# Rows of the experts gathered on TensorE by products with a 0/1 matrix, and a third set of expert weights in the space of keys and values

## What is computed

```python
t = h.reshape(-1, 1024)                           # 384 tokens
grp_gate, grp_idx = top_k(softmax(t @ moe_wg + moe_bg), 1)        # 1 of 4 groups
sel = (t @ moe_we + moe_be) of that group                         # 8 experts in a group
top_p, top_i = top_k(softmax(sel), 2)                             # 2 of the 8
w = grp_gate * top_p / sum(top_p)
for e in range(32):
    y = (silu(t @ w_gate[e]) * (t @ w_up[e])) @ w_down[e]         # hidden size 256
    acc += combine[:, e] * y
```

## Time and profile before

| what | value |
|---|---|
| median of 3 runs | 1150.37 us (1147.16 to 1150.96) |
| profiled execution, its own time | 1151.86 us |
| its span | 1150.1 us |
| PE busy / DVE / ACT / POOL | 970.8 / 487.3 / 332.5 / 138.0 us |
| mean granted clock of TensorE | 0.926 of full speed |
| DMA moved | 302.08 MB, mean 263 GB/s |
| chain that ended last | PE 51%, DMA 26%, DVE 14% |
| line of the chain with most | PE L666 26%, then the DMA of `moe_w_up` 24% |

### The profile page before, as it was taken

How to read it: one execution, slowest core, us unless ns; L and a number is a source line. 1 busy time by engine, 2 the same in 40 slices (tenths; PEclk the granted TensorE clock), 3 DMA queues, 4 the chain that set the end, 5 groups by cost and what they waited for, 6 DMA issues and landing times.

```text
span 1150.1 us, 20717 instructions
## 1 busy us (share of the span) xinstructions
PE 970.8 (84%) x7674; PEld 646.0 (56%) x7674; DVE 487.3 (42%) x1271; ACT 332.5 (29%) x879; POOL 138.0 (12%) x193
## 2 busy tenths in 40 slices
PE   5899888999468788788879999998964887888887
PEld 3456655655345455455558888776543554555454
DVE  2079876521632333333430314685145332333334
ACT  3211353530522222221330101575132222222222
POOL 0400140000400010000010055000022100010000
PEclk8999999999679999988979999998976999999998
DMA  9999736772269999999873323100215799999993
GB/s 353 279 316 361 254 110 234 264 271 74 101 229 374 416 416 417 419 418 418 337 257 110 96 87 129 56 1 2 78 69 219 298 416 417 416 417 417 417 418 126
DMA packets 84913, 302.08 MB, mean 263 GB/s; under 512 B 5541, under 2 KB 34449, under 8 KB 68465
## 3 DMA queue, kind: packets, MB, share of 16 engines
q1 hardware_dynamic: 81584, 291.03, 65.4%
q0 software_dynamic: 2832, 8.61, 2.6%
q10 hardware_dynamic: 432, 1.57, 0.3%
HBM read 291.87 MB, written 9.32 MB: 262 GB/s over the span
## 4 chain that ended last, share of the span: by engine, by line
PE 51%; DMA 26%; DVE 14%; ACT 3%; issue 3%; SPq 1%; POOL 1%; POOLq 0%; DVEq 0%; ACTq 0%
PE banks L666 26%; DMA ring<-in_moe_w_up_dram 24%; PE banks L978 6%; PE banks L675 5%; DVE a L1508 5%; PE banks L1022 4%; PE banks L973 4%; DVE a L1443 2%; PE banks L704 2%; PE banks L1001 1%; DVE rt L1443 1%; SPq L561 1%; DMA bc<-in_moe_be_dram 1%; PE banks L949 1%; POOL bc L2041 1%
## 5 line engine op out<-in xcount | busy, mean ns | idle before, releaser
L666 PE MATMUL banks<-ring,hT 128*128 128x256 f32 (+1 forms) x720 | 153.9, 376 | 1.7 <-ACT hT L1164 1.6
L666 PEld LDWEIGHTS banks<-ring,hT 128*128 128x128 f32 x720 | 135.0, 191 | 21.3 <-DMA ring<-in_ev_w_in_dram 1.9
L1216 ACT ACTIVATE a<-banks 32x256 f32<-32x256 f32 (+1 forms) x208 | 88.3, 425 | 199.0 <-PE banks L1001 100.5
L1539 DVE SCALAR_TENSOR_TENSOR xT<-banks,mod,xT 128x128 f32<-128x128 f32 x352 | 118.7, 409 | 63.0 <-PE banks L1022 63.0
L1022 PE MATMUL banks<-a 128*128 128x384 f32 x352 | 134.0, 527 | 3.5 <-ACT a L1216 3.3
L1443 DVE TENSOR_TENSOR a<-a,banks 64x128 f32<-64x128 f32 (+1 forms) x64 | 21.7, 340 | 268.9 <-ACT a L1199 268.9
L666 PE MATMUL banks<-hT,ring 128*128 128x384 f32 x384 | 127.9, 493 | 1.6 <-ACT hT L1164 1.6
L978 PE MATMUL banks<-ring,a 128*32 128x128 f32 x2560 | 92.1, 304 | 43.1 <-DMA ring<-in_moe_w_up_dram 42.5
L978 PEld LDWEIGHTS banks<-ring,a 128*32 128x32 f32 x2560 | 80.5, 122 | 69.5 <-issue 68.4
L973 PE MATMUL banks<-ring,a 128*64 128x256 f32 x704 | 85.7, 398 | 25.5 <-DMA ring<-in_moe_w_up_dram 20.4
L666 PEld LDWEIGHTS banks<-hT,ring 128*128 128x128 f32 x384 | 73.1, 192 | 53.5 <-issue 3.8
(11 more groups left out here) (262 smaller groups left out, 1038.3 us busy)
## 6 DMA issues: line engine op xcount, KB each, us to landing
ring<-in_moe_w_gate_dram SPq DMA_DIRECT2D x64, 1024.0 KB, 8.7
ring<-in_moe_w_up_dram SPq DMA_DIRECT2D x64, 1024.0 KB, 10.8
ring<-in_moe_w_down_dram SPq DMA_DIRECT2D x64, 1024.0 KB, 10.3
ring<-in_ada_w_dram SPq DMA_DIRECT2D x44, 1024.0 KB, 8.4
ring<-in_od_w_qkv_dram SPq DMA_DIRECT2D x12, 1024.0 KB, 5.5
ring<-in_ev_w_in_dram SPq DMA_DIRECT2D x6, 1024.0 KB, 12.8
a<-sorted_rows SPq DMA_DIRECT2D x12, 512.0 KB, 6.8
a<-in_ada_w_dram SPq DMA_DIRECT2D x4, 1024.0 KB, 17.6
```

The lines of the kernel that those rows point to most:

```text
L666: mm = pe.matmul(out, lhsT, rhs, start=(k == 0), stop=(k == len(pairs) - 1))
L1216: ins = act.activation(y_pair[q % BUFFERS][row:row + rows, width * b:width * b + width], work[3][rows * b:rows * b + rows, 0:width], ACT.Copy)
L1539: ins = ve.scalar_tensor_tensor(out=xT[:, c, a:b], in0=work_banks(l)[pair + k][:, a:b], scalar=mcol(l, 5, c, j), in1=xT[:, c, a:b], op0=AL ...
```

## The change

- The rows of a tile are gathered from `htok` on PE: for each of 8 chunks of channels, three products (one for each 128 tokens) with `picks`, a matrix of 0 and 1 that says which token stands in which row of the tile. Two halves of 12 products, both through `work[0]`; DVE copies half 0, ACT half 1 into `teT`.
- `picks` of tile 0 is made by DVE during routing, from expert and rank alone; those of tiles 1 to 10 by POOL, from the codes that routing makes anyway (six comparisons of 128x128 and one addition of 128x384 for a tile).
- `sorted_rows`, its scatter, its loads, `pad_stored`, the prefix sum, `starts` and POOL's copy for each expert go.
- `AHEAD` = 3: the weights of experts 2, 5, 8 ... go to `a23` (`beside_ring`), the others stay in `ring`; expert n is loaded when expert n-3 is done. Expert 2 is fixed in the first place of the sorted ones and loaded before the order is known, once the first output product of the mixer is done.
- The loop body stays at six steps, with 3 turns in place of 4; six more steps are written out.

```diff
+AHEAD = 3
-BODIES = (NE - 1 - STEPS_AHEAD) // UNROLL
+BODIES = (NE - 1 - STEPS_AHEAD) // UNROLL - 1
...
+        def expert_slot(l, n, k):
+            return beside_ring[k] if n % AHEAD == AHEAD - 1 else slot(expert_piece(l, n, k))
...
 (SP, expert_loads)
-                            sp.wait_ge(sem(used), BUFFERS * t + (NE * l + n - 1))
+                            sp.wait_ge(sem(used), AHEAD * t + (NE * l + n - AHEAD + 1))
...
-                for n in range(BUFFERS):
-                    weights(n, 0, False)
-                sp.wait_ge(sem("rows_sorted"), 16 * 2 * NT * (l + 1))
-                for i, rows in enumerate(sorted_in):
-                    sp.dma_start(rows, sorted_rows[P * i:P * i + P, :]).then_inc(sem(f"sorted{i}_loaded"), 16)
+                weights(0, 0, (0, 1))
+                is_filled(sp, ("out", l, 0))
+                sp.wait_ge(sem("cache_stored"), 32 * (l + 1))
+                weights(AHEAD - 1, 0)
+                weights(0, 0, (2,))
+                weights(1, 0)
                 sp.wait_ge(sem("order_ready"), l + 1)
...
 (PE, routing)
+                pe.wait_ge(sem("first_picked"), l + 1)
+                is_read(pe, ("htok", l, NT - 1, 1))
+                gather(opened(("rows", l, 0)), 0, 0).then_inc(sem("filled"), 1)
                 out = opened(("lead", l))
                 pe.wait_ge(sem("counts_compared"), l + 1)
                 product(out[0:NE, 0:2], [(outranks[0:NE, :], ones[0:NE, 0:2])])
-                product(out[0:NE, 2:4], [(below[0:NE, 0:NE], count_col[0:NE, :])])
                 product(out[:, NE:2 * NE], [(ones[0:NE, :], outranks[0:NE, :])], True)
+                gather(opened(("rows", l, 1)), 0, 1).then_inc(sem("filled"), 1)
...
+            def gather(out, q, half):
+                for c in range(4):
+                    for t in range(NT):
+                        mm = pe.matmul(out[:, P * c:P * c + P], htok[:, t, 4 * half + c:D:KD], picks[:, q % 2, t, :],
+                                       start=(t == 0), stop=(t == NT - 1))
+                return mm
...
 (PE, step)
                     q, i = group_step(n)
-                    if i:
+                    if i == 0:
+                        gather_half(q + 2, 0, t)
+                    else:
                         spread_out(q, ((0, 1), (2, 3))[i - 1], t)
+                        if i == 1:
+                            gather_half(q + 2, 1, t)
                     down(n - 1, t)
+                def second_step():
+                    gate_up(1)
+                    await_hid(0)
+                    hid_turn(0)
+                    gather_half(1, 0)
+                    down(0)
+                    gather_half(1, 1)
+                    pe.wait_ge(sem("diagonals_ready"), l + 1)
+                    for i in range(NT):
+                        pe.matmul(work[4 + i], ones[:, :], diagonals[:, 4 * i:4 * i + 4, :], start=True, stop=True).then_inc(sem("codes_filled"), 1)
...
 (DVE, routing; the prefix sum and the places are left out)
+                for t in range(NT):
+                    ins = ve.tensor_scalar(picks[:, 0, t, :], lane, fixed[:, t:t + 1], None, ALU.is_equal)
...
                 link(ve.memset(key_col[0:STATIC, :], -1e6))
+                link(ve.memset(key_row[:, STATIC:STATIC + 1], 4e6))
...
 (POOL)
-                    link(pool.memset(a7[0:ROWS, 0:D], 0.0))
-                    pool.dma_start(sorted_rows[PAIRS:PAIRS + ROWS, :], a7[0:ROWS, 0:D]).then_inc(sem("pad_stored"), 16)
-                    pool.wait_ge(sem("pad_stored"), 16)
...
+                pool.wait_ge(sem("codes_found"), l + 1)
+                for q in range(1, TILES):
+                    if q == 2:
+                        is_filled(pool, ("rows", l, 1))
+                    elif q > 2:
+                        pool.wait_ge(sem("rows_gathered"), 2 * (GROUPS * l + q - 2))
+                    if GROUPS * l + q > 1:
+                        pool.wait_ge(sem("picked"), GROUPS * l + q - 1)
+                    for i in range(2 * NT):
+                        ins = pool.tensor_scalar(equal[:, i, :], lane, pick_codes[:, q - 1, i:i + 1], None, ALU.is_equal)
+                    link(ins)
+                    ins = pool.tensor_tensor(out=picks[:, q % 2, :, :], in0=equal[:, 0:NT, :], in1=equal[:, NT:2 * NT, :], op=ALU.add)
+                    ins.then_inc(sem("picked"), 1)
```

## The result

The changed kernel takes **1248.78 us** (1246.15 to 1257.1, 4 runs), the kernel before 1149.51 (1147.16 to 1150.96, 4 runs): a ratio of 1.0878 [1.0824, 1.0933]. The forecast was 1135, with 1149 as its upper end, so it had the wrong sign, by 114 us. The profiled execution took 1248.54 us, 1246.8 of them span.

A forecast was written before the change was run, and what follows sets the result against it. DMA was taken to bound the experts' steady part, with PE close behind. 1151.86 - 3.3 (pad) - 10 (experts, both layers) - 2 (layer ends) = 1136.6, median 1.5 lower: 1135 us, range 1120 to 1149.

The forecast's parts named there:

- part 3: Steady expert groups: with the gather a group takes 23.3 us against DMA's 22.61; experts -5.0 us a layer, start included.
- I take 0.12: 5.8 us for a tile, 2.88 for each half: Gather on PE in the steady groups: 48 records a tile at 0.12 us each.
- PE's weight loads do not hide: Rival, gather's strided weight loads: 0.16 to 0.19 us a record, kernel 1170 to 1195 us; chance 0.10.
- the trace speaks for overlap: Gather records: load and product overlap, 0.125 us a pair by the trace, so the gather does not cost double.
- PE becomes the bound, DMA is left with room: Steady expert groups: PE at 23.3 us a group becomes the bound by a little, above DMA's 22.61.
- Part 2: Routing and start of a layer's experts: expert 2's step starts at 340, before 348.90; 8.9 us won.
- POOL beside DVE: POOL making picks of tile 1 while DVE works on the diagonals: 1.8 us added to 3.7 us.
- Part 1: Pad's store at the kernel's start removed: gains load some 7 us earlier, 3.4 kept, -3.3 us after a semaphore.
- Part 4: End of a layer, last spread after expert 31 at a higher clock: -1 us a layer, -2 in all.
- The third set: Third space for expert weights: 3 MB more loaded per layer while DMA has room, free; otherwise 7.5 us.
- three buffers instead of two hide the jitter: Steady expert groups: the third weight buffer covers jitter while PE at 23.3 us slightly exceeds DMA's 22.61; no separate gain.
- Sums: Steps of the last group, without gather: 5.1 + 6.6 + 5.9 = 17.6 us of PE, 11.9 up to expert 31.

The follow-up runs named there:

- before_product: The kernel before, with its 48 transposes of sorted rows (stride 8, stationary) made products with the identity; 1187.56 us in one run.
- moving8: before_product with operands swapped: identity stationary, the strided rows (stride 8) moving; 1184.53 us in one run.
- the stride runs: Changed kernel with the gather's stationary operand read at stride 2, 3 or 4 floats in place of 8; 1135.15, 1190.91 and 1250.69 us.
- contig: Changed kernel with token rows stored chunk by chunk, so the gather's stationary operand is 128 neighbouring floats; 1128.42 us, ratio 0.9794 to the kernel before.
- contig_again: The same kernel as contig, run again beside a version with two sets of expert weights; 1125.45 us, ratio 0.9781 to the kernel before.
- before_nopad: The kernel before without the store of the pad of zeros and its two waits; 1145.94 us, ratio 0.9953.

## Why the prediction was wrong, point by point

- **The failed step is in part 3**: "I take 0.12: 5.8 us for a tile, 2.88 for each half". A record took 0.246. It had two rows behind it: products of this shape with both operands contiguous, and transposes that read with stride 8. Each had one of the two properties of a gather record, a product and a stride, and none had both. before_product shows that the pair of them makes the price. The halves measured 5.90 + 5.58 in place of 5.76, which makes 29.0 of the 23.3 for a group; it was 28.82. Nine groups are 50 us more, and the start, with four halves at 3 us more and smaller terms against them, 9 (45.0 in place of 36). From the forecast's -5.0 a layer that makes +54; measured +55.1 and +54.2.
- **The rival** "PE's weight loads do not hide" had the place, the stride and the point from which it decides (24.2 us a group) right, and a chance of 0.10. It was priced too low, 0.19 a record at most and 1195 us, because it added the load to the product. moving8 shows that its mechanism is not the whole either: the same pace comes with the stride in the moving operand, under loads of ordinary length. The sentence that "the trace speaks for overlap" proved nothing: its row came from contiguous operands.
- **A rule left out.** The passage of the Trainium skill on 16-byte lines, cited under the stride runs, spoke against this change, and the forecast did not weigh it. It gives no size. With the doubled record that the runs show, a rival would have stood at 29 us a group, some 54 us more in each layer, and so about 1243, an estimate from 1135 and twice 54.
- **PE becomes the bound, DMA is left with room** (part 3): right in `contig`, whose groups are 22.9 us against 23.3, with DMA's share at 1.01, so that PE and DMA end nearly together. Half of the 0.4 us is the second half's tail, 2.68 in place of 2.88, under which the next record starts; the other half is 0.07 at each of the three `down`s.
- **Part 2**, without the stride: expert 0's products 13.9 us after the ranks (forecast 15.4), expert 2's step 34.1 (forecast 36). The order of events was right: two halves, experts 0 and 1, a wait for POOL's `picks`, the rest. The second half ran at a clock of 1.00, as assumed; the first at 0.60, a little above the half clock assumed, so 4.66 us in place of 5.6.
- **POOL beside DVE**: in the changed kernel six comparisons took 4.79 us while DVE did its work on the codes (the diagonals, 1.76 us with two SBUF operands, among it), and 3.49 just behind, with DVE idle:

```profile
318.48 4.79 POOL L2141 TENSOR_SCALAR a<-counting,pTbuf 128x128 f32<-128x128 f32 x6 [26.05 <-DVE pTbuf L1489]
...
324.51 3.49 POOL L2141 TENSOR_SCALAR a<-counting,pTbuf 128x128 f32<-128x128 f32 x6 [0.17 <-POOL a L2143]
```

  The added 1.8 us were 1.3, and a comparison alone is 0.58 in place of 0.43, so the sum of 5.5 stood at 5.8. The rule of the Trainium skill on the port that the two share ("SBUF — State Buffer", who interferes with whom) agrees with these rows.
- **Part 1**: -3.3 forecast. The wait for the taps did shrink by 3.27 us. The step that fell short is that only the wait counts: with it came 1.5 us of higher clock behind it, and the attention's first transpose is 6.4 us earlier in contig and contig_again, 7.1 in before_nopad. For the whole kernel the six runs of before_nopad give 3.3 to 7.5 us. The marks further on scatter: the same kernel, profiled twice (contig and contig_again), has its ranks at 300.59 and 297.72 after an attention that starts at the same time, so neither the -8.5 of the changed kernel's trace nor the -4.4 of before_nopad's is the price of the pad.
- **Part 4**: -1 a layer forecast, for a last spread at a higher clock. By the time from expert 31's gate and up to the last sums of squares ahead of the next mixer (L728 before, L733 now), layer 0 had 21.2 us before, 18.5 in the changed kernel (its spread 2.85 + 2.86 us for 8.53 before), 21.0 in `contig` and 18.5 in contig_again, the same kernel as `contig`. So -0.2 or -2.6, by whether the clock held (mean 0.84 or 1.00), and the same kernel showed both. In layer 1 the end took 26.1 us before and 26.0 to 26.1 in all three: nothing. Where -2 in all is near the trace, it is luck.
- **The third set** was costed at nothing, and its use at "three buffers instead of two hide the jitter". DMA did load it in idle time, right; what it hides is not jitter in the groups but waits in the last 12 us of a layer, 5.3 us for the two layers together.
- **Sums.** The first two steps of a group are 4.87 and 6.80 us by the forecast's own rows, not 5.1 and 6.6, so expert 31 follows the last group's start by 11.7 and not 11.9. The sum of 17.6 is right, and no conclusion hangs on the difference.

In `contig`'s trace the terms are -3.6 to the ranks of layer 0, -9.2 and -9.6 from the ranks to expert 31, -1.6 between the layers, together -24.0 against -15.3 forecast. So even without the stride the forecast was 9 us short, mostly in the experts: a group of 22.9 in place of 23.3 and a start of 34.1 in place of 36.

## What to carry to other kernels

Before a product is priced by a row of the trace, compare the access of each operand too, not only the shape: here an fp32 product that read its stationary operand with a stride of 4 or 8 floats, or its moving one with 8, cost two contiguous ones, and a transpose, which kept its pace on the same data, was no evidence for it. Where a buffer is written once and read by many products, give the stride to the copy that fills it: here one `rearrange` in ACT's copy, which takes 0.60 us for 512 columns with it or without, was worth 120 us and turned a loss of 9% into a gain of 2%. A further set of weights pays where the engine that uses them is quicker than DMA, and that can be the last group alone. A clock that holds in one execution and not in the next moves single traces by 2 to 3 us, so a term of that size wants more than one trace.

## What the hardware showed that was not expected

- The pace of a strided product did not follow the granted clock, between 0.70 and 1.00. PE in three halves of the changed kernel's gathers (length, busy, clock, DMA share):

```profile
301.04:306.98 5.94, 5.94 (x25) 5.82 (x25) 0.54 (x5) 1.18 (x3) 0.00 (x0) 0.70 0.00 0
307.46:313.37 5.91, 5.91 (x26) 5.79 (x26) 2.50 (x12) 0.00 (x0) 0.00 (x0) 0.71 0.00 0
403.17:409.07 5.90, 5.90 (x25) 5.78 (x24) 1.91 (x3) 0.48 (x2) 0.00 (x0) 1.00 0.98 362
```

  0.70 of full speed or 1.00, DMA idle or at 0.98: 5.9 us each time. The contiguous half of `contig` took 4.66 at a mean clock of 0.60 and 2.88 at 1.00. So something that the granted clock does not set holds the strided product back. That it is the reading of its operand fits the stride runs, but no run isolates it.
- The stride costs next to nothing at 2 floats and all that was ever seen from 4 on (0.120, 0.126, 0.183, 0.242, 0.246 us for 1, 2, 3, 4 and 8), in the stationary operand; in the moving one 0.236 at 8. A transpose takes 0.117 at 8, though its load record grows from 140 to 192 ns.
